# Mixture-of-experts kernel on one core: the down product with its operands exchanged

## The reference

```
def ec_moe(h, w_router, w_gate, w_up, w_down):
    aff = jax.nn.softmax(ht @ w_router, axis=-1)
    gates, idx = lax.top_k(aff.T, cap)            # cap = 2 * tokens / 16
    xs = ht[idx]
    a = jnp.einsum('ecd,edf->ecf', xs, w_gate)
    u = jnp.einsum('ecd,edf->ecf', xs, w_up)
    y = jnp.einsum('ecf,efd->ecd', jax.nn.silu(a) * u, w_down) * gates[..., None]
    out = jnp.zeros((t, d), h.dtype).at[idx.reshape(-1)].add(y.reshape(-1, d))
x = x + gate2 * ec_moe(h2)
```

## Time and profile before

| what | us |
|---|---|
| median of 3 runs | 3155.08 (3148.97 to 3156.8) |
| profiled execution, its own time | 3149.47 |
| profiled execution, span of the page | 3147.7 |
| PE busy | 2963.6 (94%) |
| DVE busy | 1970.5 (63%) |
| ACT busy | 1706.5 (54%) |
| POOL busy | 344.0 (11%) |

### The profile page before, as it was taken

How to read it: one execution, slowest core, us unless ns; L and a number is a source line. 1 busy time by engine, 2 the same in 40 slices (tenths; PEclk the granted TensorE clock), 3 DMA queues, 4 the chain that set the end, 5 groups by cost and what they waited for, 6 DMA issues and landing times. The chain is left out here.

```text
span 3147.7 us, 53853 instructions
## 1 busy us (share of the span) xinstructions
PE 2963.6 (94%) x21335; PEld 2829.0 (90%) x21335; DVE 1970.5 (63%) x2870; ACT 1706.5 (54%) x2765; POOL 344.0 (11%) x433
## 2 busy tenths in 40 slices
PE   8999998989389999999999999999999999999994
PEld 2699997768289999999999999999999999999994
DVE  1334332132557778777777877777777777777773
ACT  2322221133256666666666666666666666666663
POOL 2234332022200000000000000000000000000002
PEclk9999998989589999999999999999999999999997
DMA  8411102044378888878888887888888888888884
GB/s 321 134 38 30 36 28 69 23 165 147 100 219 260 263 255 263 265 245 273 258 262 260 259 265 247 273 257 264 260 258 266 251 269 255 264 260 261 255 261 156
DMA packets 629011, 668.59 MB, mean 212 GB/s; under 512 B 23649, under 2 KB 610225, under 8 KB 625714
## 3 DMA queue, kind: packets, MB, share of 16 engines
q1 hardware_dynamic: 621106, 644.49, 64.4%
q0 software_dynamic: 7680, 20.98, 3.1%
HBM read 633.39 MB, written 31.98 MB: 211 GB/s over the span
## 5 line engine op out<-in xcount | busy, mean ns | idle before, releaser
L1211 DVE TENSOR_TENSOR w_lo<-rawW,w_hi 128x1024 fp32r<-128x1024 f32 x1050 | 1273.8, 1223 | 232.5 <-ACT w_hi L1206 217.6
L1206 ACT ACTIVATE w_hi<-rawW 128x1024 fp32r<-128x1024 f32 x1056 | 1105.8, 1059 | 141.3 <-PE psD L1388 136.0
L1375 PE MATMUL psG<-X,w_hi 128*128 128x320 f32 x2816 | 746.9, 348 | 5.4 <-DVE X L1581 5.4
L1375 PE MATMUL psU<-X,w_hi 128*128 128x320 f32 x2816 | 743.0, 347 | 0.0
L1386 PE MATMUL psD<-hid,w_hi 128*128 128x320 f32 x2816 | 730.9, 347 | 0.0
L1377 PE MATMUL psG<-X,w_lo 128*128 128x160 f32 x2816 | 668.4, 237 | 0.0
L1388 PE MATMUL psD<-hid,w_lo 128*128 128x160 f32 x2816 | 667.2, 237 | 0.0
L1377 PE MATMUL psU<-X,w_lo 128*128 128x160 f32 x2816 | 667.1, 237 | 0.0
L1377 PEld LDWEIGHTS psG<-X,w_lo 128*128 128x128 f32 x2816 | 539.8, 192 | 0.0
L1388 PEld LDWEIGHTS psD<-hid,w_lo 128*128 128x128 f32 x2816 | 537.9, 191 | 0.0
L1377 PEld LDWEIGHTS psU<-X,w_lo 128*128 128x128 f32 x2816 | 537.9, 191 | 0.0
(11 more groups left out here) (226 smaller groups left out, 3286.9 us busy)
## 6 DMA issues: line engine op xcount, KB each, us to landing
rawW<-in_w_gate SPq DMA_DIRECT2D x352, 512.0 KB, 4.9
rawW<-in_w_up SPq DMA_DIRECT2D x352, 512.0 KB, 4.9
rawW<-in_w_down SPq DMA_DIRECT2D x320, 512.0 KB, 4.8
wm<-in_w_mod SPq DMA_DIRECT2D x24, 1024.0 KB, 5.1
rawW<-in_w_down SPq DMA_DIRECT2D x64, 256.0 KB, 4.1
raw<-in_w_in SPq DMA_DIRECT2D x32, 192.0 KB, 2.4
rawc<-catT SPq DMA_DIRECT2D x10, 512.0 KB, 5.8
acc<-x SPq DMA_DIRECT2D x10, 512.0 KB, 2.7
```

Source lines behind the costliest of these rows:

```text
L1206: act.activation(w_hi[:, n % SPLIT, :], raw[:, n % RAW, :], ACT.Copy).then_inc(f_hi, 1)
L1211: eng.tensor_tensor(w_lo[:, n % SPLIT, :], raw[:, n % RAW, :], w_hi[:, n % SPLIT, :].bitcast(F32), ALU.subtract).then_inc(f_lo, 1)
L1375: pe.matmul(out[:, f, 0:2 * C], hi[:, k, f * P:(f + 1) * P], X[:, x, :], start=(x == 0), stop=False, skip_group_check=True)
```

## The change

In the down product the operands change places. The hidden activations become the stationary operand (a 128 x 128 block: 128 hidden rows x 128 latent tokens), and the weight moves: a half is now 128 hidden rows x all 1024 output columns. For each half PE issues six float32r products of 512 moving columns into `psY` (hi x hi, lo x hi, hi x lo, two pieces of 512 each), whose result has the latent tokens on the partitions. The context tokens leave the split: their hidden values are kept in float32 (`hidc`), 128 x 32 for each block, and multiply the unsplit weight in `rawW` in four float32 products of 256 moving columns. The j-th writes partitions 32 j to 32 j + 31 of `psC`, so it uses the j-th quarter of the array's columns; in the built program these products have a tile of 128 x 32 at column 0, 32, 64 and 96, all others of the down product one of 128 x 128 at 0.

```
-        def parts(n):
...
+            if n < GU_HALVES:
...
+            else:
+                src = wd_[:, e, n - GU_HALVES, :]
+            sp.dma_start(dst, src).then_inc(f_raw[n % RAW], 16)
...
                         for n in range(RAW if first else 0, HALVES):
-                            sp.wait_ge(f_lo, HALVES * e + n - RAW + 1)
+                            sp.wait_ge(f_lo if RAW <= n < GU_HALVES + RAW else f_use, HALVES * e + n - RAW + 1)
                             load(sp, e, n)
...
-                    def down_tile(n, q):
-                        t = 4 * (n - GU_HALVES) + q
-                        f, out = t % FB, psD[t // FB % 2]
...
-                        for b in range(2):
-                            pe.matmul(out[:, b, 0:2 * C], hi[:, q, b * P:(b + 1) * P], hid[:, f, :],
...
-                            mm = pe.matmul(out[:, b, 0:C], lo[:, q, b * P:(b + 1) * P], hid[:, f, 0:C],
...
+                    def down(n):
+                        f, slot = n - GU_HALVES, n % SPLIT
+                        latent_hi, latent_lo = hid[:, f, 0:CS], hid[:, f, CS:2 * CS]
+                        for w, x in ((w_hi, latent_hi), (w_hi, latent_lo), (w_lo, latent_hi)):
+                            for half in range(2):
+                                pe.matmul(psY[:, half, :], x, w[:, slot, half * 512:(half + 1) * 512],
+                                          start=(f == 0 and w is w_hi and x is latent_hi), stop=(f == FB - 1 and w is w_lo),
+                                          skip_group_check=True)
+                        for j in range(Q4):
+                            mm = pe.matmul(psC[j * CP:(j + 1) * CP, 0:D // Q4], hidc[:, f, :],
+                                           raw[:, n % RAW, j * (D // Q4):(j + 1) * (D // Q4)],
+                                           start=(f == 0), stop=(f == FB - 1), skip_group_check=True)
                         return mm
...
-                            if i == 0 and not first:
-                                columns_to_rows(e - 1)
...
+                            if f == X_AT and not last:
+                                pe.wait_ge(f_ua, STEPS * (e + 1))
+                                rows_to_columns(e + 1)
...
+                    def y_rows(e):
+
+                        dve.wait_ge(f_use, HALVES * (e + 1))
+                        dve.wait_ge(f_si, e + 1)
+                        dve.scalar_tensor_tensor(ys[0][:], psY[:].rearrange("p b c -> p (b c)"), gc[:, 0:1], gate2[:],
+                                                 ALU.mult, ALU.mult)
+                        dve.scalar_tensor_tensor(ys[1][:], psC[:, 0:D // Q4], gc[:, 1:2], gate2c[:],
+                                                 ALU.mult, ALU.mult).then_inc(f_y, 1)
...
-                        dve.tensor_tensor(hf[:], sg[:], ua[:], ALU.mult).then_inc(f_hf, 1)
+                        dve.tensor_tensor(hidc[:, 2 * i:2 * i + 2, :], sg[:, :, CS:C], ua[:, :, CS:C], ALU.mult)
+                        dve.tensor_tensor(hf[:], sg[:, :, 0:CS], ua[:, :, 0:CS], ALU.mult).then_inc(f_hf, 1)
```

```
                 def _(act):
+                    for q in range(2):
+                        for k in range(NK):
+                            op = act.activation(diagE[:, q, k, :], ident[:], ACT.Copy, scale=modT[:, 5, k, q:q + 1])
+                    op.then_inc(e_diag, 1)
                     act.wait_ge(e_v, 2)
                     act.activation(L[:], L[:], ACT.Exp).then_inc(e_exp, 1)
                     for n in range(SPLIT):
                         half_hi(act, 0, n)
+                    act.wait_ge(e_row, 1)
+                    act.activation(gate2[:], rowE[:], ACT.Copy)
+                    act.activation(gate2c[:], rowC[:, 0:D // Q4], ACT.Copy)
```

More of the change, by code:

```diff
@@ L1166, in build @@
         GU_HALVES, HALVES = 4 * STEPS, 6 * STEPS
-        PASSES, FB = 4, FF // P
+        FB, X_AT = FF // P, 5
         RAW, SPLIT, AHEAD = 11, 6, 4
@@ L1175, in build, with load @@
         wd_ = io["w_down"][0].rearrange("e (f p) d -> p e f d", p=P)
-        def parts(n):
+        USES = [len(range(j, HALVES, RAW)) for j in range(RAW)]
+        def load(sp, e, n):
+            dst = raw[:, n % RAW, :]
             if n < GU_HALVES:
                 i, kind, half = n // 4, n // 2 % 2, n % 2
[L1181 to L1199, removed]
+                src = (wg_, wu_)[kind][:, e, 4 * half:4 * half + 4, i * W_STEP:(i + 1) * W_STEP]
+                dst = dst.rearrange("p (k f) -> p k f", k=4)
+            else:
+                src = wd_[:, e, n - GU_HALVES, :]
+            sp.dma_start(dst, src).then_inc(f_raw[n % RAW], 16)
         def half_hi(act, e, n):
-            act.wait_ge(f_raw[n % RAW], PER_EXPERT[n % RAW] * e + LANDED[n])
+            act.wait_ge(f_raw[n % RAW], 16 * (USES[n % RAW] * e + n // RAW + 1))
             if not isinstance(e, int) or HALVES * e + n >= SPLIT:
@@ L1212, in half_lo @@
                               ALU.subtract).then_inc(f_lo, 1)
+        gate2, gate2c = sb("gate2", [P, D]), sb("gate2c", [P, D // Q4])
         idxT = sb("idxT", [P, 48], I32)
@@ L1230, in build @@
                                                             sem("e_t"), sem("e_f"), sem("e_tt"))
+            onesE = sb("onesE", [P, P], F32, c)
+            diagE = sb("diagE", [P, 2, NK, P], F32, c)
+            rowE, rowC = ps("rowE", [P, D], c), ps("rowC", [P, 512], c)
+            e_ones, e_diag, e_row = sem("e_ones"), sem("e_diag"), sem("e_row")
             ROUNDS = CS // 8
@@ L1246, in _ @@
                 def _(pe):
+                    pe.wait_ge(e_ones, 1)
+                    pe.wait_ge(e_diag, 1)
+                    for k in range(NK):
+                        pe.matmul(rowE[:, k * P:(k + 1) * P], onesE[:], diagE[:, 0, k, :], start=True, stop=True)
+                    for k in range(NK):
+                        j = k // 2
+                        mm = pe.matmul(rowC[j * CP:(j + 1) * CP, k % 2 * P:(k % 2 + 1) * P], onesE[:, 0:CP],
+                                       diagE[:, 1, k, :], start=True, stop=True)
+                    mm.then_inc(e_row, 1)
                     pe.wait_ge(e_aff, 1)
@@ L1324, in build @@
             psG, psU = ps("psG", [P, 2, 512], c), ps("psU", [P, 2, 512], c)
-            psD = [ps(f"psD{i}", [P, 2, 512], c) for i in range(2)]
+            psY, psC = ps("psY", [P, 2, 512], c), ps("psC", [P, 512], c)
             f_gl, f_ul = sem("f_gl"), sem("f_ul")
@@ L1400, in rows_to_columns @@
                         mm.then_inc(f_xt, 1)
[L1402 to L1411, removed]
                     rows_to_columns(0)
@@ L1425, in body @@
                             gate_or_up(psU, e, i, 1)
-                            if i == 0 and not first:
-                                columns_to_rows(e - 1)
                         for n in range(GU_HALVES, HALVES):
+                            f = n - GU_HALVES
                             pe.wait_ge(f_lo, HALVES * e + n + 1)
[L1430 to L1442, removed]
+                            if f % 2 == 0:
+                                pe.wait_ge(f_hl, STEPS * e + f // 2 + 1)
+                            if f == 0 and not first:
+                                pe.wait_ge(f_y, e)
+                            mm = down(n)
                             mm.then_inc(f_use, 1)
+                            if f == X_AT and not last:
+                                pe.wait_ge(f_ua, STEPS * (e + 1))
+                                rows_to_columns(e + 1)
                     experts(pe, body)
-                    columns_to_rows(E - 1)
                 @block.scalar
@@ L1470, in x_hi @@
                             act.activation(X[:, a:b, 0:C], xm[:, a:b, :], ACT.Copy).then_inc(f_xh, 1)
[L1472 to L1488, removed]
                     def after_gate(e, i):
@@ L1503, in hidden_hi @@
                         act.wait_ge(f_hf, STEPS * e + i + 1)
-                        act.activation(hid[:, 2 * i:2 * i + 2, 0:C], hf[:], ACT.Copy).then_inc(f_hh, 1)
+                        act.activation(hid[:, 2 * i:2 * i + 2, 0:CS], hf[:], ACT.Copy).then_inc(f_hh, 1)
                     x_modulated(0)
@@ L1513, in body @@
                                 after_up(e, i - 1)
-                            elif not first:
-                                y_low(e - 1, PASSES - 1)
                             if not (first and i == 0):
@@ L1521, in body @@
                                 ahead_hi(e, n + 1, last)
-                            if i == 1 and not first:
-                                y_rows(e - 1)
                             after_gate(e, i)
@@ L1543, in _ @@
                     experts(act, body)
-                    y_low(E - 1, PASSES - 1)
-                    y_rows(E - 1)
                 @block.vector
@@ L1582, in x_lo @@
                                               ALU.subtract).then_inc(f_x, 1)
[L1584 to L1589, removed]
-                                                              modT[:, 5, 2 * j + b, r:r + 1], yl[:, b, a:z],
```

(17 more changed lines are left out.)

19 lines of the change are left out of this document (6 added, 13 removed).

## The result

| | us |
|---|---|
| before, median of 4 runs | 3152.94 |
| changed, median of 4 runs | 3171.47 (3169.38 to 3172.62) |
| ratio, 95% interval | 1.0058 (1.0041 to 1.0076) |

What follows compares the result with a forecast made beforehand. PE alone was taken to bound each expert. The profiled 3149.5 us plus 200 for down and 4 for routing and end gave 3353.5; with 5.6 to reach the median, 3359, range 3060 to 3400.

Steps and rivals of the forecast that it cites:

- the first rival: Down, narrow products: all quarters run at once, 0.43 us, a half 2.04, 3133 us in all, 0.7% faster; chance 0.33.
- The bound: Whole expert: PE busy for all of its 138.5 us at full clock, everything else has slack.
- the narrow products' price: Down, eight narrow instructions of a half: starts in program order, so five turns of 0.215, 1.07 us.
- the upper end: Down, narrow products of a half: nothing overlaps, 8 x 0.215 = 1.72 us.
- The wide products: Down, six float32r products of 512 columns in each half: 0.227 us each, 1.36 together.
- the break-even: Down: a half below about 2.12 us, narrow products under 0.51, would make the changed kernel faster.
- The tile change: Down, switching from wide to narrow products and back: 0.25 us in each half.
- Routing: Routing stage: ACT's 16 diagonal blocks and PE's 32 instructions delay the top-k chain, +6 us.
- The end: After PE's last down product: two DVE products replace sums, transposes and copies, -2.5 us.
- Loads, DVE and ACT: Experts: later-freed slots, DVE's and ACT's work and the splits stay hidden behind PE, costing nothing.

Runs made afterwards that it cites:

- pairs by quarter: Changed kernel with the narrow context products of two halves issued together, all of quarter 0 first, then quarter 1, and so on: 3117.1 us.

## Why the prediction was wrong

**The direction held by luck, the size did not.** With only the failed term below put right (0.445 for 1.07), the prediction's own sum gives a half of 2.055 and some 3138 us, faster than before. That the change is slower after all comes from three smaller terms of a half, each a little short (below). The range, 3060 to 3400, held because it took in the first rival. The bound (PE alone, no slack, full clock) was read rightly, and so were the terms that came from rows of the same form: an expert's change is 22 x 2.155 - 45.5 - 1.0, and with the measured half the working gives +0.9, beside the measured 1.0.

**The step that failed** is the narrow products' price, "Eight instructions then need five turns, 5 x 0.215 = 1.07". They need two, 0.445. The reason given, that PE's instructions start in program order, had been read from stretches in which all instructions share one place in the array; no row there could show the contrary, as the prediction itself said of the upper end. In its place the runs show all four quarters starting within 0.02 us, two turns for the eight, and an engine that behaves as if each quarter held four instructions, one of them running: the first instruction of the next quarter passes the second of the last. The changed kernel's own `rowC` row, 16 instructions of four quarters in 1.10 with four in a row for each quarter, is of the same kind. That error is 0.62 us in each of 352 halves, 220 us.

**What of the first rival was off** is small: full packing was forecast at 2.04 a half and 2.155 came. The wide products cost 1.40 instead of 1.36; the change of tile 0.31 instead of 0.25; the narrow ones 0.445 instead of 0.43. These 0.115 in 352 halves are 40 us, and with them the rival's 3133 becomes 3173, beside the measured 3171. The prediction put the break-even at 2.12 for a half: the measured 2.155 lies just above, and this is why the change loses.

**The tile change** was taken from the one pair of rows that had it, 0.25, and came out a quarter larger. **Routing** (+6 forecast, 6.8 measured) was late for the two reasons named, ACT's 16 blocks and PE's 32 small instructions, but the two sizes missed in opposite ways: the blocks delay the exponential by 4.8 (5.7 forecast), PE adds 2.0 where 0.5 was forecast. PE's instructions ran at a granted clock of 0.50, the 1.2 GHz level, behind 5.50 us in which PE was idle. Window of the changed kernel (columns as in the earlier trace rows):

```profile
826.00:831.30 5.30, 4.63 (x32) 4.14 (x32) 1.00 (x5) 5.27 (x8) 2.10 (x1) 0.50 1.10 350
```

**The end** (-2.5 forecast) gave -2.6. **Loads, DVE and ACT** were costed at nothing; no run shows a hole on PE in the experts, not even with six halves' slots held.

The Trainium skill, "TensorE: Matmul & The Clock Gate", Part 3, says that products on different column tiles start about 4 ns apart. The trace agrees in kind, 5 to 8 ns in the changed kernel. The Trainium skill says in the same place that matmuls start strictly in program order. Here the measurement differs: with two to four instructions for a quarter in a row, all quarters started at once (pairs by quarter: within 0.04 us). The Trainium skill, "TensorEngine Tiling (Array Packing)", Key Properties, says that changing the tiling mode drains the engine; the runs agree that the change costs time, 0.31 to 0.33 us back and forth; that it is a drain they don't show.

## What to carry to other kernels

Narrow float32 products on separate column quarters ran at once here, so price a pack at its deepest quarter, and list the instructions so that no quarter gets more than four in a row. A change between the 128 x 128 and the 128 x 32 tile cost 0.31 to 0.33 us back and forth, with 8 or with 48 narrow instructions between, so collect narrow work into few groups: here the same change went from 0.6% slower to 2.7% faster by that and by moving its small setup off a serial chain. A rule read from rows that could not have shown the contrary bounds nothing; keep its opposite as likely until a row of the right form exists.

## What the runs showed of the hardware that was not expected

A quarter of the array behaves as if it took up to four instructions, one running and three waiting (128 x 32 tiles, float32): with eight for each in a row, quarter 1 started only with the fifth of quarter 0 (0.894 after 0), with six only with the third (0.462), with four at once (0.013). And the wide products in down cost 0.233 each (1.40 for six), not the 0.227 of the earlier trace rows; why was not tried.
